# A second projection in another chunk order, with the mixers interleaved into it, and modulation sums moved into the FFN

## The reference

```python
# first block: ... its FFN, d_ff = 2816
gate, up = jnp.split(u @ w_gate_up[i], [D_FF], axis=-1)
y = (jax.nn.silu(gate) * up) @ w_down[i]
h = h + rmsnorm(y, ffn_post_norm[i])
h = h + (p[i] @ ple_proj[i]) * jax.nn.sigmoid(h @ ple_gate[i])
# second block
mod = jax.nn.silu(c) @ w_ada[l] + b_ada[l]            # 1024 x 6144 (adaLN)
sh1, sc1, gt1, sh2, sc2, gt2 = [m[:, None, :] for m in jnp.split(mod, 6, axis=-1)]
h = rms_norm(x, g_mix[l]) * (1 + sc1) + sh1
proj = h @ w_in[l]                                    # 1024 x 2576
lru_x, lru_y, q, k, v, g_out, gate_lr = jnp.split(proj, splits, axis=-1)
lru_h = rg_lru(causal_depthwise_conv(lru_x, ...), ...)       # RG-LRU
lru_out = lru_h * jax.nn.gelu(lru_y)
o = gla_chunked(q, k, v, log_alpha of gate_lr)               # GLA, 4 heads
gla_out = rms_norm(o, gla_gnorm[l]) * jax.nn.silu(g_out)
mix = jnp.concatenate([lru_out, gla_out], axis=-1) @ w_out[l]
x = x + gt1 * mix
h2 = rms_norm(x, g_ffn[l]) * (1 + sc2) + sh2
x = x + gt2 * hierarchical_moe(h2, ...)               # 32 experts, top 2 of a group
```

## Time and profile before

| | |
|---|---|
| median of 3 runs | 1054.93 us (1052.94 to 1057.79) |
| the profiled execution's own time | 1055.67 us |
| its span, first to last instruction | 1053.8 us |
| TensorE busy, mean granted clock | 839.0 us (80%), 0.907 |
| VectorE, ScalarE, GpSimd busy | 462.5, 364.9, 34.1 us |
| read from HBM | 277 MB, 264 GB/s over the span |

### The profile page before, as it was taken

How to read it: one execution, slowest core, us unless ns; L and a number is a source line. 1 busy time by engine, 2 the same in 40 slices (tenths; PEclk the granted TensorE clock), 3 DMA queues, 4 the chain that set the end, 5 groups by cost and what they waited for, 6 DMA issues and landing times. The chain is left out here.

```text
span 1053.8 us, 21560 instructions
## 1 busy us (share of the span) xinstructions
PE 839.0 (80%) x8161; PEld 669.1 (63%) x8162; DVE 462.5 (44%) x773; ACT 364.9 (35%) x511; POOL 34.1 (3%) x127
## 2 busy tenths in 40 slices
PE   5999799799999998889967788587766557686573
PEld 5999689699999997789636674343432223343231
DVE  3654886665555545653486453222311222232212
ACT  5433674365464543554463341011101010111102
POOL 3000100000000000000000000000000000000000
PEclk9999999799999998989978989988978787898877
DMA  7675240346646455256566493899999999999993
GB/s 252 209 279 191 79 144 19 119 139 221 198 160 199 159 180 153 95 185 217 223 263 220 190 389 101 327 401 426 426 428 427 426 424 428 425 427 424 426 431 145
DMA packets 88253, 278.68 MB, mean 264 GB/s; under 512 B 7279, under 2 KB 67098, under 8 KB 70810
## 3 DMA queue, kind: packets, MB, share of 16 engines
q1 hardware_dynamic: 87518, 276.84, 68.0%
q10 hardware_dynamic: 700, 1.36, 0.4%
HBM read 277.13 MB, written 1.05 MB: 264 GB/s over the span
## 5 line engine op out<-in xcount | busy, mean ns | idle before, releaser
L368 PE MATMUL bank<-R_r,Whi_r 128*128 128x256 f32 x864 | 252.5, 292 | 25.3 <-DVE R_r L1926 7.3
L369 PE MATMUL bank<-R_r,Whi_r 128*128 128x256 f32 x864 | 250.1, 289 | 0.0
L370 PE MATMUL bank<-R_r,Whi_r 128*128 128x256 f32 x752 | 217.3, 289 | 0.0
L368 PEld LDWEIGHTS bank<-R_r,Whi_r 128*128 128x128 f32 x864 | 171.5, 198 | 28.8 <-issue 24.2
L369 PEld LDWEIGHTS bank<-R_r,Whi_r 128*128 128x128 f32 x864 | 171.8, 199 | 0.1
L370 PEld LDWEIGHTS bank<-R_r,Whi_r 128*128 128x128 f32 x752 | 149.0, 198 | 0.0
L2345 DVE TENSOR_TENSOR V<-V,bank 64x256 f32<-64x256 f32 x34 | 14.4, 424 | 244.6 <-ACT V L1189 244.6
L1871 DVE TENSOR_TENSOR Whi_r<-Wlo,Whi_r 128x2048 fp32r<-128x2048 f32 x33 | 75.6, 2292 | 64.1 <-ACT Whi_r L1016 28.7
L1646 PE MATMUL bank<-Whi,S 128*32 128x256 f32 x832 | 63.9, 475 | 47.5 <-DMA Whi<-in_w_up 32.7
L299 ACT ACTIVATE Whi_r<-Wlo 128x1024 fp32r<-128x1024 f32 x68 | 67.8, 1050 | 82.6 <-PE bank L370 82.6
L308 DVE TENSOR_TENSOR Whi_r<-Wlo,Whi_r 128x1024 fp32r<-128x1024 f32 x54 | 63.6, 1221 | 59.1 <-ACT Whi_r L299 59.0
(11 more groups left out here) (456 smaller groups left out, 1464.4 us busy)
## 6 DMA issues: line engine op xcount, KB each, us to landing
Wlo<-in_w_in SPq DMA_DIRECT2D x24, 1024.0 KB, 5.2
Wlo<-in_w_gate_up SPq DMA_DIRECT2D x22, 1024.0 KB, 6.3
Whi<-in_w_gate SPq DMA_DIRECT2D x10, 2048.0 KB, 25.2
Whi<-in_w_up SPq DMA_DIRECT2D x10, 2048.0 KB, 29.7
Whi<-in_w_down SPq DMA_DIRECT2D x10, 2048.0 KB, 31.4
projR<-in_w_up SPq DMA_DIRECT2D x9, 2048.0 KB, 37.6
Wlo<-in_w_gate SPq DMA_DIRECT2D x9, 2048.0 KB, 27.8
Wlo<-in_w_up SPq DMA_DIRECT2D x9, 2048.0 KB, 32.3
```

The costliest lines, as they stand in the source:

```text
L368: pe.matmul(o, w_hi[:, c], tile(x_hi, k), start=(k == 0), stop=False)
L369: pe.matmul(o, w_hi[:, c], tile(x_lo, k), start=False, stop=False)
L370: mm = pe.matmul(o, w_lo[:, c], tile(x_hi, k), start=False, stop=(k == KT - 1))
```

## The change

- The 16 adaLN groups are loaded during the first 8 FFN rounds, two a round. VectorE multiplies each by its 128 values of silu(c) (`csil`) and adds it to a running sum per third (`ada_mac`, 2048 columns each, every second one in two halves around the gate's low part). Before the second projection TensorE adds the 128 rows of each sum, 4 matmuls for a third.
- SP's and VectorE's FFN loops are written out.
- `proj2` makes its chunks in the order LRU x (2), GLA q and k (2), v (2), LRU y (2), output gate (2). The GLA and RG-LRU steps of every engine stand between the chunks; `conv` is split by halves, and the output gate's SiLU is in its copy out of PSUM.
- GpSimd takes the added shift of the projection's input (`nmix2_shift`), three memsets, and the six GELU steps ahead of the tanh.
- The head norm is summed for each head into 32 partitions, so that root and reciprocal are 256 columns each, and four small matmuls spread the result (`og_scale`).
- The first half of `wout2` runs in two parts, the LRU rows of the mix first.

```diff
-        ADA_SLOT = (2, 3, 4, 5, 10, 11, 0, 1) + (8, 5, 11, 0, 1) * 4
-        ADA_FIRST, ADA_RING = KT, 5
-        ADA_BANK = (6, 5, 4)
+        ADA_SLOT = (2, 3, 4, 5, 10, 11, 0, 1)
+        ADA_FIRST = KT
+        ADA_BANK = (6, 5, 3)
+        ADA_REST = [(b, k) for k in range(KT) for b in range(1, ADA_B)]
+        ada_raw = [projR[:, 2 * CH:3 * CH], slot[5]]
+        ada_sum = [None, projR[:, 0:CH], projR[:, CH:2 * CH]]
...
+        def proj2_load(sp, c):
+
+            i, j = divmod(c, 2)
+            if i:
+                sp.wait_ge(*upto(f"proj2_lo{j}", i * 2))
+            at = PROJ2_ORDER[c] * 256
+            sp.dma_start(slot[proj2[3][j]].rearrange("p (k n) -> p k n", k=KT),
+                         proj2[1].rearrange("(k p) n -> p k n", p=P)[:, :, at:at + 256]
+                         ).then_inc(sem(f"proj2_full{j}"), 16)
...
+        PROJ2_ORDER = (0, 1, 4, 5, 6, 7, 2, 3, 8, 9)
...
+            def ada_rest(m):
+                b, k = ADA_REST[m]
+                if m >= 2:
+                    sp.wait_ge(*upto("ada_mac", m - 1))
+                sp.dma_start(ada_raw[m % 2], ada_w[:, k, b * CH:(b + 1) * CH]
+                             ).then_inc(sem(f"ada_raw{m % 2}"), 16)
...
+            ada_rest(0)
+            ada_rest(1)
+            for i in range(1, NF):
                 ffn_load_in(i, False)
+                if 2 * i < len(ADA_REST):
+                    ada_rest(2 * i)
                 ffn_load_out(i, False)
+                if 2 * i < len(ADA_REST):
+                    ada_rest(2 * i + 1)
+            sp.wait_ge(*upto("ada_mac", len(ADA_REST)))
...
+            def ada_mac(m, a, z):
+
+                b, k = ADA_REST[m]
+                raw, total, c = ada_raw[m % 2][:, a:z], ada_sum[b][:, a:z], csil[:, k:k + 1]
+                dve.wait_ge(*upto(f"ada_raw{m % 2}", 16 * (m // 2 + 1)))
+                if k == 0:
+                    ins = dve.tensor_scalar(total, raw, c, None, ALU.mult)
+                else:
+                    dve.wait_ge(*upto("ada_mac", m - 1))
+                    ins = dve.scalar_tensor_tensor(out=total, in0=raw, scalar=c, in1=total,
+                                                   op0=ALU.mult, op1=ALU.add)
+                if z == CH:
+                    ins.then_inc(sem("ada_mac"), 1)
...
                                   ALU.mult).then_inc(sem("gate_scaled"), 1)
+                if 2 * i < len(ADA_REST):
+                    ada_mac(2 * i, 0, CH)
+                    ada_mac(2 * i + 1, 0, HALF)
                 if not last:
                     lo(slot[0], slot_r[6], slot_r[7], "gate", i + 2)
+                if 2 * i < len(ADA_REST):
+                    ada_mac(2 * i + 1, HALF, CH)
                 lo(slot[4], slot_r[10], slot_r[11], "down", i + 1)
                 dve.wait_ge(*upto("silu_ready", i + 1))
                 dve.wait_ge(*upto("up_done", i + 1))
...
+            for b in range(2):
+                y, g = tile(projR, 4 + 2 * b, 2), tile(gel, 2 * b, 2)
+                pool.wait_ge(*upto(f"proj2_out{b}", 4))
+                pool.tensor_tensor(g, y, y, ALU.mult).then_inc(sem("gelu_a"), 1)
+                pool.wait_ge(*upto("gelu_a", 2 * b + 1))
+                pool.tensor_scalar(g, g, GELU_CUBIC, 1.0, ALU.mult, ALU.add
+                                   ).then_inc(sem("gelu_a"), 1)
+                pool.wait_ge(*upto("gelu_a", 2 * b + 2))
+                pool.tensor_tensor(g, g, y, ALU.mult).then_inc(sem("gelu_in"), 1)
 
...
+            def proj2_step(c):
+
+                i, j = divmod(c, 2)
+                act.wait_ge(*upto(f"proj2_done{j}", i + 1))
+                if c + 2 < len(PROJ2_ORDER):
+                    act_hi(act, proj2, i + 1, j)
+                proj2_out(c)
+
...
-            pe.wait_ge(*upto("nmix2_shift", KT))
+            pe.wait_ge(*upto("ada_mac", len(ADA_REST)))
+            pe.wait_ge(*upto("pgate_out1", 2))
+            for b in range(1, ADA_B):
+                for j in range(4):
+                    mm = pe.matmul(bank[ADA_BANK[b]][32 * j:32 * j + 32, :], ones[:, 0:32],
+                                   ada_sum[b][:, j * 512:(j + 1) * 512], start=True, stop=True,
+                                   skip_group_check=True)
+                mm.then_inc(sem("ada_summed"), 1)
...
+            proj2_chunk(0, lambda k: pe.wait_ge(*upto("proj2_src_lo", k + 1)))
+            proj2_chunk(1)
+            for b in range(1, ADA_B):
+                mod(b)
+            pe.wait_ge(*upto("nmix2_shift", 2))
...
                                start=True, stop=True)
             mm.then_inc(sem("ga_done"), 1)
 
-            pe.wait_ge(*upto("gv_out", 1))
-            for g in range(ADA_FIRST, ADA_FIRST + 5):
-                ada(g)
-            pe.wait_ge(*upto("conv", 4 * HT))
-            for b0, w in ((0, wrb), (2, wib)):
+            proj2_chunk(3)
+            pe.wait_ge(*upto("conv1", 8))
+            pe.wait_ge(*upto("mod_ready", ADA_B))
+            pe.wait_ge(*upto("ga", 2))
...
+            proj2_chunk(4)
+            gla_scores(0, 0)
+            proj2_chunk(5)
+            gla_scores(1, 64)
+            proj2_chunk(6)
+            gla_scores(2, P)
+            pe.wait_ge(*upto("proj2_out1", 3))
+            pe.wait_ge(*upto("lgate_out", 2 * HT))
+            for t in range(TT):
+                for c in range(4):
+                    mm = pe.transpose(bank[4 + t][:, c * P:(c + 1) * P], half(projR, 12 + c, t),
+                                      ident[:, :])
+                mm.then_inc(sem("gv_done"), 1)
+
+            proj2_chunk(7)
             pe.wait_ge(*upto("gl_out", 6))
...
                     mm.then_inc(sem("og_done"), 1)
-            pe.wait_ge(*upto("ga", 2))
-            for g in range(ADA_FIRST + 7, ADA_FIRST + 13):
-                ada(g)
+
+            proj2_chunk(8)
             for h in range(GLA_HEADS):
                 if h % 2 == 0:
                     pe.wait_ge(*upto("og_sq", h // 2 + 1))
-                mm = pe.matmul(bank[2 + h // 2][:, (h % 2) * T:(h % 2 + 1) * T], ones[:, 0:P],
-                               tile(sq, h), start=True, stop=True)
-                if h % 2:
-                    mm.then_inc(sem("og_ss"), 1)
-            for g in range(ADA_FIRST + 13, len(ADA_GROUPS)):
-                ada(g)
-            for b in range(1, ADA_B):
-                mod(b)
-            pe.wait_ge(*upto("og_rms", 2))
-            pe_dense(pe, wout2, lambda k: pe.wait_ge(*upto("wout2_src_lo", k // 2 + 1)))
+                mm = pe.matmul(bank[6][h * 32:(h + 1) * 32, T:2 * T], ones[:, 0:32],
+                               tile(og_sq, h), start=True, stop=True)
...
+            proj2_chunk(9)
+            pe.wait_ge(*upto("og_rinv"))
+            pe.wait_ge(*upto("pick_set", GLA_HEADS))
+            for h in range(GLA_HEADS):
+                mm = pe.matmul(og_scale[:, h, :], pick[h * 32:(h + 1) * 32, :],
+                               og_rms[h * 32:(h + 1) * 32, :], start=True, stop=True)
+            mm.then_inc(sem("og_rows"), 1)
+
...
+            for j in range(2):
+                pe.wait_ge(*upto(f"wout2_lo{j}", 2))
+                wout2_half(j, range(HT))
+            for j in range(2):
+                wout2_half(j, range(HT, KT)).then_inc(sem(f"wout2_done{j}"), 1)
+            for j in range(2):
+                pe.wait_ge(*upto(f"wout2_lo{j}", 4))
+                pe.wait_ge(*upto(f"wout2_out{j}", 1))
+                wout2_half(j, range(KT)).then_inc(sem(f"wout2_done{j}"), 1)
```

331 lines of the change are left out of this document (194 added, 137 removed).

## The result

The changed kernel takes 1026.04 us (median of 4 runs, 1025.63 to 1027.20), the kernel before 1054.53 (4 runs, 1052.94 to 1057.79): ratio 0.9728, interval 0.9703 to 0.9753. The profiled execution of the changed kernel took 1027.20 with a span of 1025.5.

What follows compares the result with a forecast made beforehand. DMA led the chain in the expert stage, which starts when `wout2` ends; ahead of it TensorE was full except in the mixers. FFN +10.2 us and projection with mixers -35.8 sum to -25.6, giving 1030 us, range 1020 to 1042.

Steps and rivals of the forecast that it cites:

- the loop of loads: FFN: down and gate loads with rounding and low part, 16.1 us a round, become 18.6 with a transfer between them.
- idle for 1.3 us a round: FFN, sign in the profile after: TensorE waits 1.3 us a round ahead of the gate matmuls.
- no bound: FFN: VectorE's added multiply-adds, 4.6 us on 8.70 of 16, make 13.3 of a round and don't limit it.
- slow start: Second projection: first chunk's window is 8.6 us at clock 0.70 where 5.76 would do, so 2.9 us.
- small products: Second projection with mixers: the mixers' small matmuls on TensorE, without adaLN's, take 18.6 us.
- wait for the head squares: Mixers: TensorE waits for squares queued behind two tanh and GpSimd's GELU steps; 0.5 to 2 us, 1.9 taken.
- wait for `wout2`'s second half: `wout2`: TensorE waits for the second two weight chunks, for rounding and low part; 1.9 us with handovers.
- 2.8 for each half: Mixers: GpSimd's GELU steps for one half, at 0.95 us for a step of 512 columns, take 2.8 us.
- The blocking of the two engines: Rival, interleaved stretch: GpSimd and VectorE take turns and TensorE stalls; about 1036, 1041 at twice the price; stall's chance 0.20.
- The hidden transfer: Rival, FFN: gate lands less than 1.2 us later, slack absorbs the extra load; about 1022 us; chance 0.12.
- the end that doesn't follow: Rival, expert stage: it has slack, so the time would stay near 1054 us; chance 0.03.
- a low clock through the projection: Rival, projection and `wout2`: many short pauses keep TensorE at 1.2 GHz, 62 us, time 1092 us; chance 0.05.

Runs made afterwards that it cites:

- e1: Changed kernel with both adaLN loads of a round issued ahead of the down load: 1020.59 us, ratio 0.9690 to the kernel before.
- e4: Changed kernel with adaLN loads from the third on bringing 64 of 2048 columns: 1063.15 us, total not comparable; FFN 199.11 us.
- d1: Changed kernel with both adaLN loads of a round between the down load and the next gate load: 1043.93 us, ratio 0.9896 to the kernel before.
- e3: Changed kernel with the 14 multiply-adds of groups k > 0 on one column of each piece: 1073.32 us, total not comparable; FFN 207.10 us.
- e2: Changed kernel with a round's second adaLN load behind the next gate load, ahead of up: 1020.97 us, ratio 0.9679 to the kernel before.
- d2: Kernel before, with 14 adaLN groups loaded and multiplied with 128 of 2048 columns: 1076.18 us, total not comparable; first projection matmul to first expert load 142.01 us.
- e6: Changed kernel with the six GELU steps on VectorE instead of GpSimd: 1026.36 us, ratio 0.9728 to the kernel before.
- e8: Changed kernel with both adaLN loads ahead of down, the first gate's low part first, and GELU on VectorE: 1019.68 us, ratio 0.9660 to the kernel before.
- e5: Changed kernel with all ten projection chunks ahead of the mixers' steps on TensorE, ScalarE and VectorE: 1053.86 us, ratio 1.0003 to the kernel before.
- e7: Changed kernel with both adaLN loads ahead of down and the first gate's low part ahead of the first multiply-adds: 1020.03 us, ratio 0.9671 to the kernel before.

## Why the prediction was right, point by point

**The FFN.** Forecast +10.2, measured +10.2. The mechanism was as forecast: the loop of loads took 18.59 (18.6), and gate landed 5.5 behind down in the first five rounds, though 5.8 and 6.2 in the next two. That the total agrees to a tenth is in part luck, since two parts were off and cancel. Counted from the FFN's first matmul, the first down load goes out 0.5 us later than before, not 1.3; and gate(8) follows the seventh down load by 348.15 - 332.72 = 15.4, not 14.6.

TensorE's own account looks different from the forecast "idle for 1.3 us a round". After gate(1) it pauses ahead of gate(4) to gate(8) only, 0.72 to 1.51 us. In the first rounds it had work left, because its first down product had come 2.75 us later than before and the first down load only 0.5. Its rounds take 17.28 and 17.47 at first, then five of 18.4 to 19.2, then 17.35 and 17.28, as forecast for the last ones (the loads of these rounds, 16.2 apart, were catching up). The first round costs 2.75 us up to the first down product, where 2.0 was in the sum: gate(1) stands 22.54 us behind the FFN's first matmul instead of 21.28, 1.3 later, and the rest is the low clock behind the pause of 2.28, 17 matmuls at about 0.21 us, which the sum put at nothing. 2.75 + 7.5 from the rounds make the 10.2.

e1 to e4 and d1 show the cause, not only its size: without the transfer between down and gate 8 us come back, with two there 18.3 more are lost. e3, and both orders of e1 and e2, also show that the "no bound" for VectorE's multiply-adds was right.

**The projection with the mixers.** Forecast 105.9, measured 105.4. The terms: first two chunks 15.1 instead of 11.5, so a slow start of 3.6 (2.9 forecast); small products 65.9 - 8 x 5.76 - 1.5 = 18.3 (18.6); wait for the head squares 1.5 (1.9); wait for `wout2`'s second half 0.7 (1.9); `wout2` without it 23.7 (23.0). The wait for the second half is the term most off, because I added rounding and low part end to end, 4.6 us; the low part of the first half is made beside the rounding of the second, and it takes 3.5, from 550.33 to 553.8. TensorE is busy for 102.92 of the 105.40 us, 98%, and chunk 5, which I called the tightest place, caused no wait.

**What was mis-sized.** "0.95 for one step of 512 columns" of GpSimd was 1.30 to 2.14, and "2.8 for each half" of GELU was 4.3 and 5.1 (519.02 to 523.35, 526.44 to 531.52). The blocking of the two engines, which I had as a rival at up to 11 us, was there with 4.0 us of VectorE's time. The wait for the head squares was worked out from the 2.8 and should have come out longer than 1.9; that it was 1.5 is luck, and what made up for it is open. The rival's first half came true (the two engines block each other), its second (it falls on TensorE) did not.

**What was not in the sum.** On the profiled execution's own basis the forecast was 1030.1 and 1027.2 was measured, 2.9 less. 0.6 of that is in the two terms. The other -2.2 lie in three stretches that the sum left alone: +2.6 ahead of the FFN, -3.2 between FFN and projection, -1.6 from the first expert load on. The table shows that they are not the change's. The stretch between takes 56.05 to 57.55 in seven profiles and 60.56 to 60.73 in five, and either value comes with either kind of kernel (57.55 changed and 60.58 e3; 60.72 before and 57.54 d2, whose edit lies later). The granted clock differs with it. In the changed kernel:

```profile
423.60:452.00 28.40, 23.86 (x192) 23.25 (x192) 18.97 (x23) 14.65 (x19) 1.83 (x5) 1.00 0.20 62
452.00:460.30 8.30, 5.58 (x33) 3.41 (x33) 3.97 (x7) 3.71 (x8) 0.51 (x2) 1.00 0.93 298
```

In e3, whose code is the same there, it was 0.88 from 421.20 to 449.60 and 0.85 in the 11.3 us that follow, so 39.7 us where the changed kernel took 36.7. In the kernel before it was 0.89 from 410.80 to 440.7 and 0.74 in the 9.9 us that follow. What sets the one or the other is open, and the clock doesn't explain all: the two runs with 56.05 differ from those with 57.5 ahead of these windows. The end stage varies between 459.7 and 461.6, the start of the FFN between 193.0 and 196.5, for kernels that are alike there. So the last 2 us are as likely chance as effect, and these runs can't settle it.

**The rivals.** The hidden transfer, the end that doesn't follow and a low clock through the projection did not come; a low clock of 17 matmuls behind one pause did. That the end follows is seen in all the profiles: the span's end stands 459.7 to 461.6 us behind the first expert load in each run with whole modulation sums.

## What to carry to other kernels

Where loads go through one queue and a loop of loads has 1 us of slack, the place of an extra transfer decides whether its size costs anything: put it ahead of or behind two transfers that are waited for together, not between them, and work out the loop's length (landing, rounding, low part) before choosing. Here 1 MB a round between down and gate cost about 8 us over seven rounds, and with it beside the two TensorE's rounds stayed at 17.28. Work put into an engine's pauses is free until the pauses are filled. Interleaving two stages pays by the pauses that it closes, 17.3 us here, and by the higher clock of the matmuls that stood among them, 9.5; taking work out of pauses alone paid nothing (d2). An operation moved to GpSimd can also take time from VectorE, 4.0 us here, so look at what lies under the bound engine before counting it as relief or as loss.

## What was not expected of the hardware

The clock granted to the same instructions differed between executions of kernels that are alike up to there: the stretch between FFN and projection took 60.6 us in e2, e3, e6 and 60.7 in e8, 57.5 in the changed kernel, e1, e4 and e5, and 56.05 in e7 and d1, with 0.88 and 0.85 in e3 where the changed kernel had 1.00. With most of adaLN's matmuls out of TensorE's pauses (d2) the mean granted clock of the stretch was lower, 0.84 instead of 0.90, and the matmuls that were left took 3.8 us longer. GpSimd's 512 columns took 1.30 us, more than half of the 1.89 for 1024, so by these two, as an estimate, about 0.7 us of its price does not depend on the columns.
